# Attention scores computed by column pieces, and three steps per head moved one or two turns later, in an f32 decoder trunk on one core

## The reference

```python
for i in range(S // Q_BLOCK):                       # 8 blocks of 128 queries
    end = (i + 1) * Q_BLOCK
    s = jnp.einsum("bqhcd,bkhcd->bhcqk", q_blk, k_pre) * scale   # c: two components
    p = jax.nn.softmax(s + bias[None, :, None], axis=-1)
    attn = p[:, :, 0] - lam * p[:, :, 1]
    outs.append(jnp.einsum("bhqk,bkhe->bqhe", attn, v_pre))
o = rmsnorm(o, subln_g) * (1.0 - lambda_init)       # per head, 128 values
return o.reshape(B, S, V_WIDTH) @ w_o
```

## Time and profile before

| | |
|---|---|
| median of 3 runs | 2421.97 us (2421.73 to 2422.86) |
| the profiled execution: its own time | 2422.19 us |
| its span from the first to the last instruction | 2420.4 us |
| mean granted TensorE clock | 0.994 |
| PE busy | 2357.6 us (97%) |
| DVE busy | 1396.2 us (58%) |
| ACT busy | 800.2 us (33%) |
| POOL busy | 69.8 us (3%) |
| chain that ended last: PE, DVE, ACT | 88%, 7%, 3% |

### The profile page before, as it was taken

How to read it: one execution, slowest core, us unless ns; L and a number is a source line. 1 busy time by engine, 2 the same in 40 slices (tenths; PEclk the granted TensorE clock), 3 DMA queues, 4 the chain that set the end, 5 groups by cost and what they waited for, 6 DMA issues and landing times.

```text
span 2420.4 us, 27168 instructions
## 1 busy us (share of the span) xinstructions
PE 2357.6 (97%) x10989; PEld 1915.2 (79%) x10989; DVE 1396.2 (58%) x2145; ACT 800.2 (33%) x1381; POOL 69.8 (3%) x51
## 2 busy tenths in 40 slices
PE   7999989999999999999999999899999999999998
PEld 6875778888788888887777777777888888888888
DVE  6996699998556544446666666665633332233234
ACT  5312432222444322224555555643411121121122
POOL 0000000000000000012011110000000000000000
PEclk9999999999999999999999999999999999999999
DMA  4110323333233333331111111211111111211112
GB/s 136 44 39 14 87 70 96 96 92 101 80 101 96 98 96 96 96 96 44 35 36 36 35 35 34 68 40 35 53 44 53 53 48 50 60 42 46 53 44 79
DMA packets 278010, 154.63 MB, mean 64 GB/s; under 512 B 5669, under 2 KB 273278, under 8 KB 277886
## 3 DMA queue, kind: packets, MB, share of 16 engines
q1 hardware_dynamic: 277886, 152.90, 21.5%
HBM read 145.54 MB, written 7.34 MB: 63 GB/s over the span
## 4 chain that ended last, share of the span: by engine, by line
PE 88%; DVE 7%; ACT 3%; issue 1%; SPq 0%; DMA 0%; DVEq 0%; ACTq 0%
PE ps L1772 27%; PE ps L1621 19%; PE ps L1623 18%; PE ps L1622 18%; PE ps L1604 3%; DVE cacc L1189 2%; DVE cvA L1189 1%; PE ps L1724 1%; PE ps L1686 1%; ACT ojunk L1002 1%; ACT sc L964 0%; DVE Wl L1114 0%; ACT L1009 0%; PE ps L1676 0%; DVE sc L1435 0%
## 5 line engine op out<-in xcount | busy, mean ns | idle before, releaser
L1621 PE MATMUL ps<-Sh,Wl 128*128 128x512 f32 x1616 | 657.1, 407 | 20.0 <-DVE Sl L1272 7.2
L1623 PE MATMUL ps<-Sh,Wh 128*128 128x512 f32 x1616 | 632.8, 392 | 0.0
L1622 PE MATMUL ps<-Sl,Wh 128*128 128x512 f32 x1616 | 632.2, 391 | 0.0
L1621 PEld LDWEIGHTS ps<-Sh,Wl 128*128 128x128 f32 x1616 | 305.4, 189 | 98.5 <-issue 27.9
L1623 PEld LDWEIGHTS ps<-Sh,Wh 128*128 128x128 f32 x1616 | 304.8, 189 | 65.8
L1622 PEld LDWEIGHTS ps<-Sl,Wh 128*128 128x128 f32 x1616 | 305.7, 189 | 60.3 <-issue 3.8
L1114 DVE TENSOR_TENSOR Wl<-raw,Wh 128x1024 fp32r<-128x1024 f32 (+2 forms) x238 | 280.5, 1179 | 125.5 <-ACT Wh L750 124.6
L750 ACT ACTIVATE Wh<-raw 128x1024 fp32r<-128x1024 f32 (+2 forms) x238 | 240.9, 1015 | 294.9 <-DMA raw<-in_ffn_w_dram 136.9
L1772 PE MATMUL ps<-Sh,Wl 128*128 128x512 f32 x688 | 212.6, 390 | 2.5 <-DVE Sl L1350 2.4
L1772 PE MATMUL ps<-Sl,Wh 128*128 128x512 f32 x688 | 211.9, 389 | 0.0
L1772 PE MATMUL ps<-Sh,Wh 128*128 128x512 f32 x688 | 211.8, 389 | 0.0
(11 more groups left out here) (196 smaller groups left out, 3179.7 us busy)
## 6 DMA issues: line engine op xcount, KB each, us to landing
raw<-in_ffn_w_dram SPq DMA_DIRECT2D x148, 512.0 KB, 3.8
raw<-in_pw_w_dram SPq DMA_DIRECT2D x32, 512.0 KB, 3.9
raw<-in_ffn_w_dram SPq DMA_DIRECT2D x32, 448.0 KB, 3.7
raw<-in_ffn_w_dram SPq DMA_DIRECT2D x24, 384.0 KB, 3.3
xrow<-in_x_dram SPq DMA_DIRECT2D x8, 512.0 KB, 6.2
raw<-in_w_q_dram SPq DMA_DIRECT2D x8, 512.0 KB, 4.9
raw<-in_w_k_dram SPq DMA_DIRECT2D x8, 512.0 KB, 6.1
raw<-in_w_v_dram SPq DMA_DIRECT2D x8, 512.0 KB, 4.1
```

Of the source, the lines that this page charges most:

```text
L1621: pe.matmul(dst, ll, rh, start=start, stop=False)
L1622: pe.matmul(dst, lh, rl, start=False, stop=False)
L1623: return pe.matmul(dst, lh, rh, start=False, stop=stop)
```

## The change

Two things are edited. First, `scores` runs over the pieces in the outer loop and over the two components in the inner one, so that the order of rows 4 to 7 becomes piece 0 of component 0, piece 0 of component 1, piece 1 of component 0, piece 1 of component 1. The waits and the counts of `s_mm` keep their meaning. Second, in the heads before the last one the root of the head behind moves from row 1 to row 2 on ScalarE and its norm from row 2 to row 3 on VectorE; and in heads 0 to 5 the high part of the value weights moves from row 1 to row 3 on ScalarE and their low part from row 2 to row 4 on VectorE. In head 6 the value weights' split stays, and in head 7 nothing moves.

```diff
@@ scalar program, row(h, i)
                 if i == 1 and h:
                     out_squares(h - 1, 1)
-                    out_root(h - 1, 4 if h == LAST else 0, TB)
+                if i == (1 if last else 2) and h:
+                    out_root(h - 1, 4 if last else 0, TB)
...
-                if i == 1 and not last:
+                if i == (1 if h == LAST - 1 else 3) and not last:
                     att_split(h + 1, V_R)
@@ vector program, row(h, i)
-                if i == 2 and not last:
+                if i == (2 if h == LAST - 1 else 4) and not last:
                     att_lo(h + 1, V_R)
                 if i == 6 and h < LAST - 1:
                     att_lo(h + 2, Q_R)
-                if i == 2 and h:
+                if i == (2 if last else 3) and h:
                     out_norm(h - 1, 4 if last else 0, TB, h if last else h - 1)
@@ tensor program, scores(t)
-                for c in range(2):
-                    cp = slice(c * HD, (c + 1) * HD)
-                    if t:
-                        pe.wait_ge(s_ev, 2 * t - 1 + c)
-                    for n0 in range(0, (i + 1) * P, HT):
-                        n1 = min((i + 1) * P, n0 + HT)
+                for n0 in range(0, (i + 1) * P, HT):
+                    n1 = min((i + 1) * P, n0 + HT)
+                    for c in range(2):
+                        cp = slice(c * HD, (c + 1) * HD)
+                        if t and n0 == 0:
+                            pe.wait_ge(s_ev, 2 * t - 1 + c)
                         ins = product(ps[:, 2 + 2 * c + n0 // HT, 0:n1 - n0], Qh[cp, qs], Ql[cp, qs],
                                       Kh[cp, n0:n1], Kl[cp, n0:n1], True, True)
-                    ins.then_inc(s_mm, 1)
+                        if n1 == (i + 1) * P:
+                            ins.then_inc(s_mm, 1)
```

## The result

The changed kernel takes 2399.84 us (median of 4 runs, 2399.29 to 2400.49), the kernel before beside it 2422.39 (4 runs, 2421.73 to 2422.86). The ratio is 0.9907, with a 95% interval of 0.9893 to 0.9922: 22.6 us faster, where 27.2 had been forecast. The time lies inside the range, 4.8 us above the value named. The profiled execution took 2400.49 us, its span is 2398.7 us, its mean granted clock 0.994.

The account below looks back on a forecast made before the run. TensorE was taken to bound the attention stage, busy 58.2 of 60.0 us per head. Scores 16.2, head 7 1.5 and stall 9.5 make 27.2 us: 2422.2 - 27.2 = 2395.0 us, range 2391.5 to 2405.

Parts of the forecast that it names:

- Scores: Rows 4 to 7: both components' pieces start together, saving 0.58 us per row, 16.2 us over seven heads.
- strict program order: Rival: score matmuls start strictly in program order, so only 9.5 us is won and 1 lost: 2413.7 us, chance 0.06.
- pieces that serialise: Rival: in the scores, alternating halves for different banks wait for each other, 19 us lost: 2431.7 us, chance 0.04.
- Stall: TensorE's wait for row 3's attention weights in heads 1 to 6 goes: 6 x 1.59 = 9.5 us.
- the first rival: Moved root or norm makes TensorE wait again by as much in row 3 or 4: 2404.5 us, chance 0.08.
- I cost these at nothing: The moved root, norm and value weights' high and low parts have cover in their new rows: no cost.
- the sentence on the queues: The key weights' load waits for the value weights' low part, so it moves from 1204.40 to about 1210, with cover.
- over 15 us: Cover claimed for the delayed key weights' transfer and one gain multiply, before bias work at 1228.34 and use at 1234.65.
- the narrowest turn: Row 5: weights ready 6.09 us behind row 4's turn, TensorE comes at 6.78, so 0.7 us to spare.
- Head 7: Nothing moves there; rows 4 and 5 save 0.58 us each, row 3 about 0.3: about 1.5 us.
- The 0.3 of row 3: Last head's turn of row 3 starts at 1587.03, its weights are ready at 1586.66: only about 0.3 us won.

Follow-up runs that it names:

- split back: The changed kernel with the value weights' split in its old rows 1 and 2 in every head, root and norm still moved: 2395.79 us, ratio 0.9891.
- multiply held: The changed kernel plus one wait: GpSimd's key weights' multiply starts only when row 5's attention weights are done: 2396.53 us, ratio 0.9893.
- scores alone: The kernel before with only the new order of the scores; root, norm and value weights' split in their old rows: 2411.47 us, ratio 0.9957.
- last root later: The split back kernel, with head 7 issuing head 6's root behind row 1's high parts of transposed weights and output weights: 2393.06 us, ratio 0.9884.
- moves alone: The changed kernel with the old order of the scores; root, norm and value weights' split stay moved: 2412.03 us, ratio 0.9958.

## Why the prediction was right, and where it was short

The sign, both mechanisms and their places were right; 27.2 us became 22.6, and the difference has addresses. By the profiled executions, whose spans differ by 21.7 us (each line is the difference of distances between turns):

| stretch | forecast | measured |
|---|---|---|
| up to the first turn | 0 | 0.9 |
| head 0 | 2.3 | 1.8 |
| heads 1 to 5 | 5 x 3.91 = 19.6 | 15.7 (3.09 to 3.22 each) |
| head 6 | 3.9 | 3.9 |
| head 7 | 1.5 | 0.9 |
| behind the attention | 0 | -1.6 |
| sum | 27.2 | 21.7 |

**Scores: right.** 0.58 us in each row of 4 to 7, whatever the width of the second piece. The rivals of strict program order and of pieces that serialise are out: row 4 would have stayed near 1.76 us or gone to 2.15, and it takes 1.18; the kernel with only this edit wins 10.3 us. In the profile of the changed kernel the first matmuls of both components are one merged pair in each piece. As in the earlier trace rows, this goes against the rule of program order without reordering that the Trainium skill gives (TensorE: Matmul & The Clock Gate, Part 3, The mechanism).

**Stall: right.** 5.19 us from turn to turn against a forecast of 5.2. The exponentials and VectorE's attention weights keep out of TensorE's way in rows 3 and 4 in every head, so the first rival (the same stall with a new owner, 2404.5) did not come about as it was described. It did come about in a smaller form, in a row where it had not been looked for.

**"I cost these at nothing": this step failed**, for one of the moved steps. The value weights' low part had a place to go in row 4, as was said, and on VectorE it costs nothing there. What was wrong is the sentence on the queues. It was seen that the key weights' load moves by some 5 us, and its cover was worked out as "over 15 us", against the engines that *use* those weights. Not asked was what the multiply would *run beside*. In the kernel before it is over at 1213.15 (the last line of this document's last fence), 4.5 us ahead of the attention weights of row 5; the load that moved by 5 us puts it on top of them. Of the narrowest turn it was said that 0.7 us was to spare in row 5; the instruction became 1.46 us longer and TensorE waited 0.67, which fits. Over heads 0 to 5 this is 0.5 + 3.8 = 4.3 us. The kernels with the split back and with the multiply held measure the same term by medians, 4.1 and 3.3 us (3.4 and 2.7 if each is taken against the kernel before beside it). Both land near the forecast (2395.79 and 2396.53 against 2395.0): with this one term corrected the sum was within 2 us.

**Head 7: mis-sized.** Rows 4 and 5 gave what was said. The 0.3 of row 3 was not won: the scores of row 4 used to cover most of another wait ahead of that turn, for the low part of the output weights. That is half of the 0.6 that is missing. The other half lies between the turn of row 2 and the scores of row 4, 4.87 us where it was 4.57: the half clock behind the wait of 4.7 us lasts until 2.05 us behind the turn of row 2, where it was 1.5 before.

```profile
1563.47 0.50 PE L1622 MATMUL ps<-Sh,Wl 128*128 128x512 f32 x1 [0.60 <-DVE Wl L1391]
...
1594.57 0.44 PE L1605 MATMUL ps<-ident,sc 128*128 128x128 f32 x2 [2.05 <-DVE sc L1436]
```

The first line is that wait, 0.60 us, with the same line of code as the wait of 4.7 us before it; the waits of before have one for this line, the changed kernel two. The second is the turn of row 6, which waits 0.56 us longer than in the earlier trace rows, as forecast.

**The clock: not in the sum.** In the profiled execution of the changed kernel a stretch behind the attention is at the lower level. Windows, before the fall and in it:

```profile
1657.80:1661.20 3.40, 0.98 (x4) 0.34 (x2) 2.61 (x4) 2.06 (x4) 0.00 (x0) 1.00 0.00 0
1661.30:1664.50 3.20, 3.13 (x7) 2.48 (x8) 3.20 (x6) 3.20 (x6) 0.00 (x0) 0.50 0.02 5
```

TensorE is busy for 0.98 of 3.4 us, then its clock is 0.50 for 3.2 us. The same wait, 2.42 us, is in all nine traces; a stretch at half clock follows it in four (the changed kernel, scores alone, split back, last root later) and not in the other five, so it doesn't go with either edit. Such a stretch costs about 1.5 us, as much as the differences between executions of one kernel here. That it comes and goes between executions of the same kernel isn't shown: each kernel has one trace.

## What to carry to other kernels

When a step is moved, follow what it releases through the queues to the end, and ask of the last thing released not only when it is needed but what will be running on the neighbouring engine at its new time: a multiply with 15 us to spare cost 4 us because it landed on the one instruction with 0.7 us to spare. A saving of matmul time in front of a turn that waits is worth nothing until the wait is gone, so a change of two parts is to be summed in both orders. If a chain is late, move first what is longest and wanted last (here root and norm), and move nothing more than the wait needs.

## What the runs showed of the hardware

Two engines exclude each other for a whole instruction, wherever they meet in these traces. GpSimd's multiply of two SBUF tensors (1.90 us) and VectorE's operations on two SBUF tensors don't overlap: whichever starts second is recorded as running, but ends only about its own time after the end of the first (VectorE's 1.02 became 2.48, ending 0.81 behind the multiply; GpSimd's 1.90 became 2.68, ending 1.76 behind VectorE). In the kernel with the moves alone another VectorE operation, the low part of the value weights, is first by 0.29 us, and the query weights' multiply again ends 1.76 behind it:

```profile
1209.32 1.22 DVE L1383 TENSOR_TENSOR Wl<-raw,Wh 128x1024 fp32r<-128x1024 f32 x1
...
1209.61 2.69 POOL L674 TENSOR_TENSOR raw<-raw,vec 128x1024 f32<-128x1024 f32 x1 [33.87 <-DMA raw<-in_w_q_dram]
```

Once the first has ended, the one that was waiting goes before the next instruction of the first one's engine (2.49 for the second multiply). The kernel before had it already, unnoticed: its two multiplies last 4.21 us in one row where they take 3.75 when nothing meets them, having met the attention weights of row 4.

```profile
1208.65 0.89 DVE L1435 SCALAR_TENSOR_TENSOR sc<-sc,small,sc 128x640 f32<-128x640 f32 x1
...
1208.94 4.21 POOL L674 TENSOR_TENSOR raw<-raw,vec 128x1024 f32<-128x1024 f32 x2 [33.21 <-DMA raw<-in_w_q_dram]
```

VectorE's instructions that read PSUM and one SBUF tensor are not slowed beside the same multiply (1.08 us for the scores, with the multiply held), nor do they slow it. The Trainium skill (GPSIMD Engine Reference, 1. Specifications) says that the two engines share SBUF interfaces and contend when VectorE reads two SBUF inputs. The traces agree, and show its size: not a shared rate but a standstill until the other's instruction is over.

Matmuls of the two halves of the array overlap across the program's order, but only over a short distance: with pieces of both components next to each other they start within a hundredth of a microsecond, with all six of component 0 ahead in the program, component 1 joined at the third. So what was said of the kernel at the start, that nothing reorders the work at run time, doesn't hold for these matmuls. Over the four longest rows of seven heads that distance was worth 16 us (28 x 0.57).
